# Transposed input, column vectors and long weight rows at the start of a one-core transformer kernel

## The reference, cut to what matters

```python
act_lat, act_ctx = silu(c), silu(c_ctx)
sh_l, sc_l, gt_l = split(act_lat @ w_ada[i] + b_ada[i], 3)      # 1024 x 3072 weights
sh_c, sc_c, gt_c = split(act_ctx @ w_ada[i] + b_ada[i], 3)
u_lat = rms_norm(x, norm_g[i]) * (1.0 + sc_l) + sh_l            # 512 tokens
u_ctx = rms_norm(ctx, norm_g[i]) * (1.0 + sc_c) + sh_c          # 256 tokens
p_lat = u_lat @ w_in                                            # query, key/value, rope and gate columns
p_ctx = u_ctx @ w_in[:, kv_lo:pe_hi]                            # key/value and rope columns alone
```

## Time and profile before

| | |
|---|---|
| median of 3 runs | 1284.62 us (1284.25 to 1284.8) |
| the profiled execution | 1285.15 us |
| its span in the profile | 1283.4 us |
| TensorE busy | 1271.1 us, 99% |
| TensorE's granted clock | 1.00, at the higher of its two levels (2.4 GHz) |
| moved by DMA | 135.43 MB |

### The profile page before, as it was taken

One profiled execution on the slowest core, in us unless ns is written; L12 is line 12 of the kernel. 1 busy time (PEld: TensorE's weight loads), 2 busy tenths in 40 slices (PEclk: granted clock), 3 DMA queues, 4 the chain that ended last, 5 costly groups with the idle time before them and its releaser, 6 DMA issues.

```text
span 1283.4 us, 17458 instructions
## 1 busy us (share of the span) xinstructions
PE 1271.1 (99%) x6553; PEld 1065.3 (83%) x6553; DVE 818.3 (64%) x1208; ACT 655.3 (51%) x1066; POOL 448.8 (35%) x212
## 2 busy tenths in 40 slices
PE   9999999999999999999999999999999999999998
PEld 4688888889988888888789889888888888888886
DVE  1796788764945457789658335406448678667686
ACT  5543777744523354766655534632355534545341
POOL 0243011137433394522244334344663322333210
PEclk9999999999999999999999999999999999999999
DMA  9972001076332153322223233233354233332301
GB/s 348 322 241 75 11 23 33 18 246 187 97 99 66 34 164 99 99 53 63 65 70 96 83 82 83 78 93 94 96 164 154 84 124 99 107 107 82 115 1 66
DMA packets 181401, 135.43 MB, mean 106 GB/s; under 512 B 10154, under 2 KB 154651, under 8 KB 181324
## 3 DMA queue, kind: packets, MB, share of 16 engines
q1 hardware_dynamic: 181122, 134.34, 34.5%
q10 hardware_dynamic: 202, 0.06, 0.0%
HBM read 129.66 MB, written 4.72 MB: 105 GB/s over the span
## 4 chain that ended last, share of the span: by engine, by line
PE 88%; DVE 4%; ACT 4%; DMA 2%; POOL 1%; issue 1%; ACTq 0%; DVEq 0%; SPq 0%; POOLq 0%
PE psum L2379 27%; PE psum L2381 26%; PE psum L2380 26%; PE psum L2437 2%; PE psum L2593 2%; DMA w_raw<-in_fno_w_in 1%; PE psum L2581 1%; PE psum L2582 1%; POOL w_lo L784 1%; ACT w_hi L903 1%; DVE m_probs L2031 1%; DVE m_turned_lo L2036 0%; PE psum L2530 0%; DMA w_raw<-in_mla_w_out 0%; DMA vec_rows<-in_moba_k_norm_g 0%
## 5 line engine op out<-in xcount | busy, mean ns | idle before, releaser
L784 POOL TENSOR_TENSOR w_lo<-w_raw,w_hi 128x1024 fp32r<-128x1024 f32 x148 | 383.6, 2598 | 641.0 <-ACT w_hi L903 605.7
L2379 PE MATMUL psum<-u_hi,w_hi 128*128 128x512 f32 (+1 forms) x704 | 265.2, 377 | 1.0 <-DVE u_lo L1837 0.6
L2381 PE MATMUL psum<-u_hi,w_lo 128*128 128x512 f32 (+1 forms) x704 | 260.9, 371 | 0.0
L2380 PE MATMUL psum<-u_lo,w_hi 128*128 128x512 f32 (+1 forms) x704 | 260.7, 370 | 0.0
L903 ACT ACTIVATE w_hi<-w_raw 128x1024 fp32r<-128x1024 f32 x148 | 155.0, 1053 | 72.2 <-PE psum L2381 28.1
L2379 PE MATMUL psum<-y_hi,w_hi 128*128 128x512 f32 x416 | 162.2, 390 | 0.0
L2381 PE MATMUL psum<-y_hi,w_lo 128*128 128x512 f32 x416 | 161.9, 389 | 0.0
L2380 PE MATMUL psum<-y_lo,w_hi 128*128 128x512 f32 x416 | 161.9, 389 | 0.0
L2379 PEld LDWEIGHTS psum<-u_hi,w_hi 128*128 128x128 f32 x704 | 132.8, 189 | 23.5 <-POOL w_lo L784 1.2
L2381 PEld LDWEIGHTS psum<-u_hi,w_lo 128*128 128x128 f32 x704 | 132.6, 188 | 23.2
L2380 PEld LDWEIGHTS psum<-u_lo,w_hi 128*128 128x128 f32 x704 | 132.9, 189 | 21.0 <-issue 0.2
(11 more groups left out here) (511 smaller groups left out, 2591.2 us busy)
## 6 DMA issues: line engine op xcount, KB each, us to landing
w_raw<-in_w_in SPq DMA_DIRECT2D x52, 512.0 KB, 3.8
w_raw<-in_w_up SPq DMA_DIRECT2D x32, 512.0 KB, 4.1
down_set<-in_w_down SPq DMA_DIRECT2D x32, 512.0 KB, 4.8
ada_back<-in_w_ada SPq DMA_DIRECT2D x7, 2048.0 KB, 11.2
w_raw<-in_fno_w_in SPq DMA_DIRECT2D x16, 512.0 KB, 3.9
ada_w<-in_w_ada SPq DMA_DIRECT2D x3, 2048.0 KB, 14.3
w_raw<-in_mla_w_in SPq DMA_DIRECT2D x11, 512.0 KB, 5.2
w_raw<-in_mla_w_out SPq DMA_DIRECT2D x8, 512.0 KB, 3.9
```

The source lines that it names most:

```text
L784: pool.tensor_tensor(WL[:, j, :], RAW[:, j % 2, :], f(WH[:, j, :]), ALU.subtract).then_inc(lo_done, 1)
L2379: pe.matmul(out, ah, bh, start=first, stop=False, skip_group_check=more)
L2380: pe.matmul(out, ah, bl, start=False, stop=False, skip_group_check=more)
L2381: return pe.matmul(out, al, bh, start=False, stop=last, skip_group_check=more)
```

## The change

The host now passes `x` and the context turned (features by tokens), the vectors as one table of 128 by 115 (`in_columns`), and `w_ada` as `[layer, quarter, partition, chunk, 512]`, so that each partition's part of a quarter is one run of 16 KB (before: eight of 2 KB).

* Loads on SyncE now go: columns, quarter 0 in halves, quarter 2, `x` in halves straight into `HT` (runs of 2 KB), weight tile 0, quarter 1, weight tile 1, quarter 3 in halves, the context (`CTX`, runs of 1 KB). The small tables and the identity are issued by ScalarE.
* All transposes of `x`, the vectors and the context are gone. The squares are made over features: four ScalarE instructions of 128x1024 (`XSQ`), four additions on VectorE (`XSUM`), four small products with ones on TensorE, and the square root over their PSUM. For the context: two ScalarE instructions, three additions (`CSUM`), one product with ones of 256 columns, the square root and a reciprocal over 128x256 (`CRSTD`).
* Weight tile 0 is split (`split_hi(A0, None, 0)`) ahead of quarter 1 instead of behind it.
* On TensorE, tile products stand between halves of quarter 3.

Its core (the host's part and the renamed semaphores are left out):

```diff
-            ada_row_copy(1, 2, 2)
+            for n in range(4):
+                x_squares(n)
+            ada_row_copy(1, 2, 2)
+            split_hi(A0, None, 0)
+            act.wait_ge(spread_mm, 2)
+            act.activation(RSC[:, 0:TT], bank(0, 2 * TT)..., ACT.Sqrt, ...).then_inc(in_sq, 1)
             act.wait_ge(s_adaq[1], 16)
...
             split_hi(A0, None, 2)
-            act.wait_ge(row_ss, 9)
-            for m in range(TC // P):
-                act.activation(CTOK[:, m, :], CTOK[:, m, :], ACT.Copy, scale=RSC[:, TT + m:TT + m + 1]).then_inc(x_scaled, 1)
+            act.wait_ge(spread_mm, 4)
+            act.activation(CRSTD[:], bank(6, TC), ACT.Sqrt, scale=1.0 / D, bias=EPST[:]).then_inc(in_sq, 1)
             act.wait_ge(kv_raw[1], 16)
             split_hi(A0, None, 3)
```

VectorE:

```diff
+            for n in range(2):
+                v.wait_ge(in_sq, 2 * n + 2)
+                a, b = slice(4 * n, 4 * n + 2), slice(4 * n + 2, 4 * n + 4)
+                link(v.tensor_tensor(XSQ[:, a, :], XSQ[:, a, :], XSQ[:, b, :], ALU.add))
+            link(v.tensor_tensor(XSQ[:, 0:2, :], XSQ[:, 0:2, :], XSQ[:, 4:6, :], ALU.add))
+            v.tensor_tensor(XSUM[:], XSQ[:, 0, :], XSQ[:, 1, :], ALU.add).then_inc(in_sum, 1)
+            v.wait_ge(in_sq, 5)
+            link(v.reciprocal(RSC[:, 0:TT], RSC[:, 0:TT]))
             for m in range(TT):
                 v.tensor_scalar(DIAG[:, m, :], IDENT[:], RSC[:, m:m + 1], None, ALU.mult)
...
+            v.wait_ge(in_sq, 7)
+            link(v.tensor_tensor(CSQ[:, 0:4, :], CSQ[:, 0:4, :], CSQ[:, 4:8, :], ALU.add))
+            link(v.tensor_tensor(CSQ[:, 0:2, :], CSQ[:, 0:2, :], CSQ[:, 2:4, :], ALU.add))
+            v.tensor_tensor(CSUM[:], CSQ[:, 0, :], CSQ[:, 1, :], ALU.add).then_inc(in_sum, 1)
...
             def ctx_chunks():
+                v.wait_ge(in_sq, 8)
+                link(v.reciprocal(CRSTD[:], CRSTD[:]))
```

TensorE:

```diff
-            ada(3)
+            pe.wait_ge(lo_done, 1)
+            pe.wait_ge(in_sq, 5)
+            ada(3, 0, 4)
+            for k in range(4):
+                pe.wait_ge(u0_lo, k + 1)
+                lat_step(0, k)
+            ada(3, 4, KC)
             pe.wait_ge(lo_done, 2)
-            for k in range(KC):
+            for k in range(4):
+                lat_step(1, k)
+                if k == 1:
+                    pe.wait_ge(mod_done, 1)
+                    last_columns()
+            for k in range(4, KC):
                 pe.wait_ge(u0_lo, k + 1)
                 for j in range(2):
                     mm = lat_step(j, k)
-                if k == 0:
-                    pe.wait_ge(mod_done, 1)
-                    last_columns()
             for j in range(2, 4):
                 pe.wait_ge(lo_done, j + 1)
                 for k in range(KC):
                     mm = lat_step(j, k)
-                    if j == 3:
-                        turn_ctx(k)
+                if j == 2:
+                    pe.wait_ge(in_sum, 2)
+                    pe.wait_ge(u0_hi, KC)
+                    pe.matmul(bank(6, TC), ONES[:], CSUM[:], start=True, stop=True).then_inc(spread_mm, 1)
```

More of the change, by code:

```diff
@@ L640, in _ @@
             key_rope_tile()
-            sp.wait_ge(row_ss, TT + 1)
-            sp.wait_ge(x_t, KC)
+            sp.wait_ge(in_sum, 2)
             gate_load(1)
@@ L927, in _, with x_squares @@
             act.activation(CSPLIT[:, :, 0:2], CACT[:], ACT.Copy).then_inc(cact_done, 1)
[L928 to L939, removed]
+            act.activation(DUMMY[:, 0:1], EPST[:], ACT.Sqrt)
+            def x_squares(n):
+                act.wait_ge(s_x[n // 2], 16)
+                act.activation(XSQ[:, 2 * n:2 * n + 2, :], HT[:, 2 * n:2 * n + 2, :], ACT.Square).then_inc(in_sq, 1)
             def ada_row_copy(n, q, done):
@@ L963, in _ @@
             act.wait_ge(s_ctx, 16)
-            for m in range(TC // P):
[L965 to L968, removed]
+            act.wait_ge(in_sum, 1)
+            for n in range(2):
+                act.activation(CSQ[:, 4 * n:4 * n + 4, :], CTX[:, 4 * n:4 * n + 4, :], ACT.Square).then_inc(in_sq, 1)
             for c in range(4, KC):
@@ L1617, in _ @@
                 if half == 0:
-                    v.wait_ge(spread_mm, 2)
-                    v.wait_ge(x_copied, KC)
+                    v.wait_ge(spread_mm, 3)
                 first_modulation(half)
@@ L2457, in _ @@
             ada(2)
-            pe.wait_ge(diag_done, TT)
+            pe.wait_ge(s_const, 16)
+            turn_row(0, 0)
+            turn_row(1, 2).then_inc(ada_mm, 1)
+            pe.wait_ge(in_sum, 1)
+            pe.wait_ge(bias_row, 3)
+            for m in range(TT):
+                mm = pe.matmul(bank(0, 2, 2 * m), XSUM[:, m * P:(m + 1) * P], ONES[:, 0:2], start=True, stop=True)
+            mm.then_inc(spread_mm, 1)
+            pe.wait_ge(q_lo1, TT)
             for m in range(TT):
@@ L3155 @@
         if name in vec_of:
-            key = vec_of[name]
-            a = a.reshape(-1, MD if key in ("q_norm", "k_norm") else P)
+            vectors[vec_of[name]] = a.reshape(-1, MD if vec_of[name] in ("q_norm", "k_norm") else P)
+            continue
+        if name in ("x", "ctx"):
+            a = _np.ascontiguousarray(a.reshape(-1, D).T)
+        elif name == "w_ada":
+            a = _np.ascontiguousarray(a.reshape(2, KC, P, 6, T).transpose(0, 3, 2, 1, 4))
         elif a.ndim == 3 and a.shape[0] == 1:
@@ L3161 @@
         d[key] = nc.dram_tensor(f"in_{name}", a.shape, _mybir.dt.from_np(a.dtype), kind="ExternalInput").ap()
+    rows = [_np.tile(vectors[name], (1, 2)) if name in ("q_norm", "k_norm") else vectors[name] for name, _ in VECS]
+    arrays["in_columns"] = _np.ascontiguousarray(_np.concatenate(rows).T)
+    d["columns"] = nc.dram_tensor("in_columns", (P, NROWS), _mybir.dt.float32, kind="ExternalInput").ap()
     for name, a in shape_constants().items():
```

151 lines of the change are left out of this document (52 added, 99 removed).

## The result

The changed kernel takes 1293.99 us (median of 4 runs, 1293.04 to 1295.67) against 1284.63 us before (1284.25 to 1284.8): 1.0075 times as long, 95% interval 1.006 to 1.009. The prediction was 1290.0 us, range 1286.9 to 1293.0: the sign is right, and the time is 1.0 us above the range and 4.0 us above the forecast. The four executions lie in two pairs, 1293.04 and 1293.15, 1294.84 and 1295.67, so the median stands between them. The profiled execution is the fastest of them, 1293.04 us; its span is 1291.2 us, 7.8 us more than before.

A forecast was written before the change was run, and what follows sets the result against it. The prediction took TensorE, busy 99% of the span, to bound the kernel, and how soon it comes through the start to set the end. Seven terms summed to +5.4 us: 1290.0 us on the median, range 1286.9 to 1293.0.

The forecast's parts named there:

- Clock (rival, 12%): TensorE's clock halves behind new pauses before the sums and tile 3: 4.3 us for both, 1292 to 1294.4; 12%.
- the likeliest case: The forecast with both costs, at the front and before tile 3: 1289.2 to 1291.5 us; 52%.
- Term 1: Front, end of quarter 1 on TensorE: +0.8 us, between -1.2 and +1.5.
- The meeting: At the front, GpSimd's first low part and VectorE's additions of squares take turns, delaying the last addition; bounds 0 and 2.4 us.
- no meeting: GpSimd asks before the squares are done or after the additions: Term 1 becomes -0.4 to -1.2, about 1288.5 us; 22%.
- Term 2: Quarter 3 in halves: last columns come after six tile steps, so TensorE waits for chunk 4's low part: +1.9 us.
- Terms 3 and 4: Tiles 2 and 3: 16 context transposes go, -1.8 us; one product with ones of 256 columns comes, +0.4 us.
- Term 5: Before tile 3: ScalarE's split queues behind the context's sum and square root, so TensorE waits for the low part: +4.0 us.
- Term 6: Behind tile 3: TensorE waits for VectorE's last context chunk: +0.5 us, between 0 and 1.5.
- Term 7: Near 282 to 321 us: later quarters of `w_ada` load faster, -0.4 us, between 0 and -1.0.
- Swallowed later: TensorE's 9.07 us of waits after 128 us absorb the delay of 5.8 us: 1284.2 us; 9%.

The follow-up runs named there:

- every pause filled: Changed kernel with unused products of ones in all four of TensorE's pauses, the waits themselves kept: 1289.77 us, 1.0033 times before.
- tile 3 early: Changed kernel with ScalarE's high part of weight tile 3 moved ahead of its wait for the context's sum and the square root: 1295.88 us.
- the three repairs: Changed kernel with the context's chain moved earlier, GpSimd's first low part held until VectorE's last addition of input squares, quarter 3 whole: 1283.94 us.
- the fastest kernel: The three repairs plus eight unused products of ones before the sums of squares and eight before the diagonals' spread: 1282.26 us, 0.9972 times before.
- the same with short rows: The fastest kernel with `w_ada` in the layout of the kernel before (2 KB pieces), all twelve quarters: 1282.88 us, 0.9981 times before.
- the kernel with the front filled: Changed kernel with unused products of ones in the front's pauses, sixteen before the sums of squares, six before the diagonals' spread: 1292.32 us.

## Why the prediction was right in its sign and wrong in its size

**Clock (rival, 12%): this is what failed.** The step was the choice of the likeliest case: the sum was made at full clock, and the two pauses it found itself were priced at no more than their length. Measured, the half clock costs 2.1 us at quarter 1 (37.27 against 35.19 with every pause filled), 1.4 us at tile 3 (6.95 against 5.57), and 3.2 to 4.2 us of the time. The rival had 4.3 us for both pauses and a time of 1292 to 1294.4; 1293.99 lies in it. Its rule, a half clock for as long as the pause, was an assumption: at the front the record read 0.50 for nearly 7 us, behind pauses of 4.0 and 1.5. The Trainium skill, "TensorE: Matmul & The Clock Gate", part 1, says that idleness puts TensorE back to 1.2 GHz; by that rule, as the prediction said, this was the forecast, and the runs agree with it.

**Term 1, quarter 1 (+0.8): +0.3 at full clock, +2.4 in fact.** The meeting is there in the predicted place (GpSimd asked at 24.09, 24.2 predicted; the addition ended at 27.44, 28.1 predicted), and without it quarter 3 starts at 33.67 instead of 35.19. The two SBUF inputs of the addition were the right thing to look for, though no run varies them: the Trainium skill, "SBUF — State Buffer", section "Who interferes with whom", states the lock, and 2.71 against 0.69 us is its price here. The rival "no meeting" is refuted. Loads came earlier than priced: the long rows moved at 425 GB/s from 4 to 9 us, quarter 1 landed at 26.8 instead of 28.2.

**Term 2, quarter 3 in halves (+1.9): +2.5.** The wait is 1.8; the other 0.7 are 0.3 for the one more change between quarter and tile, and the edges of the wait.

**Terms 3 and 4 (-1.8, +0.4): -1.6 and +0.4.** Tile 3 takes 5.57 us at full clock (every pause filled) where 5.45 was reckoned, and the new product 0.43.

**Term 5, tile 3 behind the context's sum (+4.0): 3.9**, shown by the kernel in which it goes. But the prediction didn't see that the late split was also what kept GpSimd off VectorE's second addition. Alone, undoing it gains nothing.

**Term 6, context chunks (+0.5): 0.** TensorE left tile 3 at 76.1 instead of 72.4, and the chunks were ready when it wanted them, though the last low part ended 1.2 us later than reckoned. The chain is close behind, as the kernel with tile 3 early showed (3.1 us of waits for it).

Together: 2.4 + 2.5 - 1.6 + 0.4 + 3.9 + 1.4 (the half clock at tile 3) = 9.0 us at the sums, as measured, where 5.8 were predicted. Without the half clock it is 5.6 (75.52 against 69.96). There misses of about half a microsecond cancel, terms 1 and 6 too high, terms 2 and 3 too low, and that is the luck in the agreement with 1290.0.

**Term 7 (-0.4): about -1.0, and probably not for the reason given.** The shift of 9.0 us is still there at the residual update, 291.22 against 282.24, and is 8.0 at the last one of that stage. VectorE's timeline, changed kernel, then the kernel before:

```profile
291.22 0.75 DVE L1811 SCALAR_TENSOR_TENSOR residual<-psum,ada_lat,residual 128x512 f32<-128x512 f32 x1 [4.38 <-PE psum L2371]
...
324.89 0.88 DVE L1827 SCALAR_TENSOR_TENSOR u_lo<-psum,ada_lat,u_hi 128x256 fp32r<-128x256 f32 x2 [1.00 <-ACT u_hi L1125]
325.68 0.48 DVE L1811 SCALAR_TENSOR_TENSOR residual<-psum,ada_lat,residual 128x256 f32<-128x256 f32 x1
```

```profile
316.88 0.88 DVE L1837 SCALAR_TENSOR_TENSOR u_lo<-psum,ada_lat,u_hi 128x256 fp32r<-128x256 f32 x2 [1.88 <-ACT u_hi L1140]
317.67 0.47 DVE L1821 SCALAR_TENSOR_TENSOR residual<-psum,ada_lat,residual 128x256 f32<-128x256 f32 x1
```

Nearly all of this is a shorter wait of ScalarE for a weight tile's load, 0.79 instead of 1.67 us. Faster quarters are one reading, and the runs speak against it: between the same two instructions the three repairs, with long rows, got nothing back, the fastest kernel 0.5, the same with short rows 0.7, the kernel before with long rows 1.2, and "tile 3 early", with long rows, lost 0.4. The stretch varies by such amounts with when its loads meet, and the layout doesn't sort it. What sets it stays open.

**Swallowed later (9%): no.** At most about 1.2 of 9.0 us came back. (The prediction's own threshold for this rival was off: with term 7 in the sum, 2.8 and not 3.2 us swallowed lead from 1290.0 to 1287.2.)

## What to carry to other kernels

A new wait on the bounding engine has two prices: its length, and what the half clock takes from the work behind it. Here that was 3 to 4 us on pauses of 11.2 us in all. Price it whenever a change opens pauses in an engine that was hardly ever idle, and don't count on filling one of them, for the drop moves to the next. When work is moved to VectorE additions with two SBUF inputs (in the kernel before, ScalarE alone summed the squares), look at once for what GpSimd does at that time. And when a wait is undone, ask what it was holding apart.

## What was unexpected of the hardware

* The granted clock fell behind pauses of 1.5 us (diagonals) and 1.8 us (chunk 4) as well, when other pauses stood ahead of them or had been filled in part. The 1.8 us pause cost nothing in the changed kernel (1.00 from 35 to 69 us) and did in the kernel with the front filled (0.62 from 52 to 56 us). Products of 128 columns whose results nobody reads kept it up: 1.00 to 128 us.
* While it was down, TensorE's records filled the stretch (3.00 busy of 3.00 us from 32 to 35 us) and the clock still read 0.57: a full engine doesn't mean a fast one.
* Longer DMA rows made a kernel slower: in its profiled execution the rate was 426 instead of 389 GB/s, and the small loads of another queue landed 1.6 us later.
